# One 512-column product for the high weights of A11 and A12, with VectorE adding the two halves of the bank

## The reference, cut to what matters

```python
D_MODEL, SEQ, DEPTH = 1024, 512, 4
D_FF = int(math.ceil(8 * D_MODEL / 3 / 256) * 256)      # 2816

def _swiglu(x, w13, w2):
    h = x @ w13                       # (512, 1024) @ (1024, 5632)
    g, u = jnp.split(h, 2, axis=-1)
    return (jax.nn.silu(g) * u) @ w2

for i in range(DEPTH):
    ...
    x = _layer_norm(ALPHA * x + h, ln1_g[i], ln1_b[i])
    x = _layer_norm(ALPHA * x + _swiglu(x, ffn_w13[i], ffn_w2[i]), ln2_g[i], ln2_b[i])
```

## Time and profile before

| | |
|---|---|
| median of three runs | 2151.86 us |
| lowest and highest | 2151.69 and 2152.13 us |
| span of the profiled execution | 2150.7 us |
| PE busy | 2136.8 us, 99% |
| DVE busy | 1505.6 us, 70% |
| ACT busy | 904.9 us, 42% |
| POOL busy | 551.6 us, 26% |
| matmuls of 256 columns in the seven products (L1577 to L1579) | 3 x 2016 |
| granted TensorE clock | 0.999 of full |

### The profile page before, as it was taken

One profiled execution on the slowest core, in us unless ns is written; L12 is line 12 of the kernel. 1 busy time (PEld: TensorE's weight loads), 2 busy tenths in 40 slices (PEclk: granted clock), 3 DMA queues, 4 the chain that ended last, 5 costly groups with the idle time before them and its releaser, 6 DMA issues.

```text
span 2150.7 us, 35581 instructions
## 1 busy us (share of the span) xinstructions
PE 2136.8 (99%) x13496; PEld 1898.5 (88%) x13497; DVE 1505.6 (70%) x2118; ACT 904.9 (42%) x1594; POOL 551.6 (26%) x386
## 2 busy tenths in 40 slices
PE   9999999999999999999999999999999999999998
PEld 7777899998888988999888899988887778999987
DVE  3788688873489979888544888853538868888534
ACT  3455444442233424444323445432335554454422
POOL 0000056630030002666120166610000001666100
PEclk9999999999999999999999999999999999999999
DMA  6211323433333012343521333432232113333321
GB/s 215 69 58 51 107 81 104 113 110 116 107 99 98 1 59 79 101 116 99 177 98 50 98 99 100 117 121 96 78 117 69 49 58 100 99 99 111 126 98 59
DMA packets 256749, 204.39 MB, mean 95 GB/s; under 512 B 6256, under 2 KB 235760, under 8 KB 256608
## 3 DMA queue, kind: packets, MB, share of 16 engines
q1 hardware_dynamic: 252976, 189.42, 29.2%
q0 software_dynamic: 3632, 13.02, 1.8%
HBM read 200.32 MB, written 2.10 MB: 94 GB/s over the span
## 4 chain that ended last, share of the span: by engine, by line
PE 93%; DVE 5%; DMA 1%; issue 1%; ACT 1%; POOL 0%; DVEq 0%; POOLq 0%; SPq 0%; ACTq 0%
PE ps L1498 17%; PE ps L1500 17%; PE ps L1499 17%; PE ps L1577 11%; PE ps L1578 11%; PE ps L1579 11%; DVE hid L1263 3%; PE ps L1795 2%; PE ps L1822 2%; PE ps L1623 1%; PE ps L1807 1%; PE ps L1798 1%; PE ps L1956 0%; PE ps L2051 0%; DMA raw<-in_w 0%
## 5 line engine op out<-in xcount | busy, mean ns | idle before, releaser
L963 DVE TENSOR_TENSOR w_lo<-raw,w_hi 128x1024 fp32r<-128x1024 f32 x196 | 243.1, 1247 | 333.3 <-ACT w_hi L586 332.4
L586 ACT ACTIVATE w_hi<-raw 128x1024 fp32r<-128x1024 f32 x196 | 203.5, 1055 | 373.5 <-PE ps L1500 360.0
L1577 PE MATMUL ps<-t_hi,w_hi 128*128 128x256 f32 x1152 | 326.2, 283 | 0.2 <-DVE w_lo L1404 0.2
L1578 PE MATMUL ps<-t_lo,w_hi 128*128 128x256 f32 x1152 | 326.0, 283 | 0.0
L1579 PE MATMUL ps<-t_hi,w_lo 128*128 128x256 f32 x1152 | 326.0, 283 | 0.0
L1498 PE MATMUL ps<-w_hi,a_hi 128*128 128x512 f32 x832 | 325.9, 392 | 0.0
L1500 PE MATMUL ps<-w_hi,a_lo 128*128 128x512 f32 x832 | 323.9, 389 | 0.0
L1499 PE MATMUL ps<-w_lo,a_hi 128*128 128x512 f32 x832 | 323.8, 389 | 0.0
L653 ACT ACTIVATE w_hi<-raw 128x512 fp32r<-128x512 f32 (+1 forms) x288 | 212.5, 738 | 250.3 <-PE ps L1579 235.3
L1404 DVE TENSOR_TENSOR w_lo<-raw,w_hi 128x512 fp32r<-128x512 f32 (+1 forms) x288 | 268.1, 932 | 47.3 <-ACT w_hi L653 47.1
L1577 PE MATMUL ps<-xT_hi,w_hi 128*128 128x256 f32 x864 | 244.6, 283 | 0.0
(11 more groups left out here) (170 smaller groups left out, 4223.6 us busy)
## 6 DMA issues: line engine op xcount, KB each, us to landing
raw<-in_w SPq DMA_DIRECT2D x264, 512.0 KB, 4.1
raw<-in_wqkv SPq DMA_DIRECT2D x48, 512.0 KB, 3.8
raw<-in_pw SPq DMA_DIRECT2D x24, 512.0 KB, 4.2
raw<-in_wo SPq DMA_DIRECT2D x16, 512.0 KB, 3.2
ln_gb<-in_g POOLq DMA_DIRECT2D x8, 512.0 KB, 4.3
ln_gb<-in_b POOLq DMA_DIRECT2D x8, 512.0 KB, 5.6
x_nat<-in_x SPq DMA_DIRECT2D x4, 512.0 KB, 5.4
out<-x_nat SPq DMA_DIRECT2D x3, 512.0 KB, 2.7
```

What stands on the lines that cost most here:

```text
L586: nc.scalar.activation(weight_hi(u), raw[:, r, :], ACT.Copy).then_inc(w_hi_done, 1)
L963: nc.vector.tensor_tensor(weight_lo(u), raw[:, r, :], weight_hi(u).bitcast(f32), ALU.subtract).then_inc(w_lo_done, 1)
L1577: ms = [nc.tensor.matmul(dst, hi[:, at], x_hi, start=k == 0 and f in ("A11", "S1", "S2"), stop=False, skip_group_check=True), nc.tensor.ma ...
L1578: nc.tensor.matmul(dst, hi[:, at], x_lo, start=False, stop=False, skip_group_check=True),
```

## The change

The tiles `xT_hi` and `xT_lo` become the two halves of one tile `xT`. For A11 and A12 the two matmuls with high weights (256 columns of high tokens, 256 columns of low tokens) become one matmul of 512 columns: the product with the high tokens goes to columns 0 to 255 of bank X, that with the low tokens to columns 256 to 511. The third matmul (low weights, high tokens) still adds to columns 0 to 255. The two halves of the bank must be added afterwards: ACT copies the second half to SBUF, DVE adds the first half to it (`fold_first` for A11, `fold_head` for A12). Silu for the first 256 tokens then can't be applied by that copy, so ACT applies it later to all 512 tokens at once (`all_tokens`).

```diff
             def keep_first(p):
                 act.wait_ge(form_used, used(i, p, "A11"))
                 ...
-                nc.scalar.activation(sums_kept(i)[0][:, p % 2, :], ps[:, seven_bank(i), 0:HALF], ACT.Copy).then_inc(kept, 1)
+                nc.scalar.activation(sums_kept(i)[0][:, p % 2, :], ps[:, seven_bank(i), HALF:SEQ], ACT.Copy).then_inc(kept_half, 1)
             def first_tokens(p):
                 ...
-                nc.scalar.activation(gate[:, c % 2, 0:HALF], ps[:, seven_bank(i), 0:HALF], func).then_inc(head_done, 1)
-            def last_tokens(p):
+                nc.scalar.activation(gate[:, c % 2, 0:HALF], ps[:, seven_bank(i), HALF:SEQ], ACT.Copy).then_inc(head_half, 1)
+            def all_tokens(p):
                 c = SEVEN_FROM + p
+                act.wait_ge(head_done, SEVENS * i + p + 1)
                 act.wait_ge(c12_done, SEVENS * i + p + 1)
-                nc.scalar.activation(gate[:, c % 2, HALF:SEQ], gate[:, c % 2, HALF:SEQ], func).then_inc(gate_done, 1)
+                nc.scalar.activation(gate[:, c % 2, :], gate[:, c % 2, :], func).then_inc(gate_done, 1)
...
+            def fold_first(p):
+                dve.wait_ge(kept_half, SEVENS * i + p + 1)
+                nc.vector.tensor_tensor(firsts[:, p % 2, :], firsts[:, p % 2, :], ps[:, X, 0:HALF], ALU.add).then_inc(kept, 1)
+            def fold_head(p):
+                c = SEVEN_FROM + p
+                dve.wait_ge(head_half, SEVENS * i + p + 1)
+                nc.vector.tensor_tensor(gate[:, c % 2, 0:HALF], gate[:, c % 2, 0:HALF], ps[:, X, 0:HALF], ALU.add).then_inc(head_done, 1)
...
             form_low(0, G_S1)
+            fold_first(0)
+            fold_head(0)
             make_u2(0)
             for p in range(1, SEVENS):
                 ...
                 make_c21(p - 1)
+                fold_first(p)
                 form_low(p, G_A22)
                 make_c12(p - 1)
                 form_low(p, G_S4)
                 gating_seven(p - 1)
+                fold_head(p)
                 make_u2(p)
...
+                    if f in ("A11", "A12"):
+                        both = xT[:, :, k + (4 if f == "A12" else 0), 0:HALF]
+                        ms = [nc.tensor.matmul(ps[:, X, :].rearrange("p (h n) -> p h n", h=2), hi[:, at], both,
+                                               start=k == 0 and f == "A11", stop=False, skip_group_check=True),
+                              nc.tensor.matmul(dst, lo[:, at], both[:, 0, :], start=False, stop=k == 3, skip_group_check=True)]
```

More of the change, by code:

```diff
@@ L208, in build @@
     x_nat = sb("x_nat", [P, TB, D])
-    xT_hi = sb("xT_hi", [P, KD, SEQ], f32r)
-    xT_lo = sb("xT_lo", [P, KD, SEQ], f32r)
+    xT = sb("xT", [P, 2, KD, SEQ], f32r)
+    xT_hi, xT_lo = xT[:, 0, :, :], xT[:, 1, :, :]
     hid = sb("hid", [P, FC * SEQ])
@@ L321, in build @@
     form_lo = [sem(f"form_lo{g}") for g in range(5)]
+    kept_half, head_half = sem("kept_half"), sem("head_half")
     u2_done, u3_done, c22_done, c21_done, c12_done = (sem("u2_done"), sem("u3_done"), sem("c22_done"), sem("c21_done"),
@@ L696, in up @@
                     form_high(p, G_S4)
-                    last_tokens(p - 1)
+                    all_tokens(p - 1)
                     first_tokens(p)
@@ L703, in up @@
                 split_w(after + 1)
-                last_tokens(last)
+                all_tokens(last)
                 act.wait_ge(form_used, used(i, last, "S4"))
@@ L1575, in product @@
                     at = slice(k * P, (k + 1) * P)
+                    if f in ("A11", "A12"):
[3 more added lines that the diff above has]
+                              nc.tensor.matmul(dst, lo[:, at], both[:, 0, :], start=False, stop=k == 3, skip_group_check=True)]
+                        if k < 2 and (p, f) == (SEVENS - 1, "A11"):
+                            for m, done in zip(ms, ((w_hi_done, w_lo_done), (w_used,))[k]):
+                                m.then_inc(done, 2 * SEVENS)
+                        continue
                     x_hi, x_lo = tokens(f, k)
@@ L1579, in product @@
                           nc.tensor.matmul(dst, lo[:, at], x_hi, start=False, stop=k == 3, skip_group_check=True)]
-                    if k == 0 and (p, f) == (SEVENS - 1, "A11"):
-                        for m, done in zip(ms, (w_hi_done, w_lo_done, w_used)):
-                            m.then_inc(done, 2 * SEVENS)
                 ms[-1].then_inc(form_used, 1)
```

## The result

The changed kernel took 2172.30, 2173.32, 2174.00 and 2177.19 us, median 2173.66; the kernel before 2151.99 (median of four: the three runs of the table and one more; 2151.69 to 2154.25). The ratio is 1.0101, 95% interval 1.0087 to 1.0116: slower by 1%. The profiled execution took 2172.3 us with a span of 2170.5, against 2150.7 before, so its trace has 19.8 us to account for.

The account below looks back on a forecast made before the run. TensorE was taken to bound the kernel, 93% of the chain that ended last. 12.2 - 0.4 + 7.5 + 1.0 = +20.3 us on the profiled 2150.7 gave 2171.0, as a median of runs 2172 us; range 2161 to 2184.

Parts of the forecast that it names:

- S3 waits for u2 in the held pairs: Before S3 in 64 pairs: second fold delays u2 by 0.34 us, TensorE stands 0.30, pair 10.27 not 10.08: +12.2 us.
- The gating's end is tied to T0 by POOL: DVE's gating, held until POOL is through, ends at 7.94 us after T0, A11(p)'s first matmul; the 0.107 us gain is lost.
- Last pairs: Last pair of each layer: its gating isn't held, so it keeps the merge's gain: 4 x 0.107, -0.4 us.
- First pairs: First pair of each layer: A12(0) waits for the first fold behind the low part of S1; 1.9 us each, +7.5 us.
- Load ahead of the low part: Where a load arrives before DVE's low part, POOL goes first and DVE is held 1.2 us; +1 us allowed.
- rival B: POOL's first sum often precedes the low part of S2 and S3: 0.40 us more every second pair, 2184 us; chance 0.16.
- The merge's gain: A11 and A12: two steps of 0.120 us become one of 0.227, 0.107 a pair, 7.7 us if nothing waits.
- Rival A: Gating isn't held, the second fold is free, the 7.7 us come through: 2144 us, or 2150.5 by the skill; chance 0.06.
- Rival C: u2's reserve before S3 is larger than read, folds cost only at the layers' start: -7.3 + 7.5, 2152 us; chance 0.06.

Follow-up runs that it names:

- e2: The kernel before, products not merged, with one more addition of the folds' form directly ahead of u2 in pairs 1 to 17: 2168.10 us (1.0072).
- e3: The changed kernel with the second fold moved behind u2 in pairs 1 to 17: 2157.61 us (1.0023).
- e6: The changed kernel with POOL's first sum of a pair waiting for the low part of S2 and S3 of the pair before: 2183.46 us (1.0144).
- e7: The changed kernel with the second fold and u2 ahead of the gating in pairs 1 to 17: 2156.92 us (1.0022).
- e4: The changed kernel, each layer's first pair reordered: first fold before the low part of S1, gating behind it, second fold behind u2: 2168.43 us (1.0073).
- e1: The kernel before with only the merge into 512-column products; nothing folded, low-token part of A11 and A12 left out: 2147.54 us (0.9978).
- e5: The kernel of e1 with the 512 columns read as one piece instead of two pieces of 256: 2147.32 us (0.9976).
- e9: The changed kernel with the orders of e7 and e4, A11 and A12 issued as four wide then four narrow matmuls: 2145.35 us (0.9969).

## Why the prediction was right, and which terms were off

The forecast was 2172 us, range 2161 to 2184, and the median is 2173.7. Term by term:

- **S3 waits for u2 in the held pairs.** This was the step that carried the forecast, and it was right. Predicted: u2 at T0 + 8.20, S3 first at + 8.76 (8.83 in effect), pair 10.27. Measured: + 8.19, + 8.75, 10.253. Shown by e2 (the addition alone makes the same pair) and e3 (moving it away undoes it). Predicted +12.2 us, measured 64 x 0.173 = 11.1. The step before S3 was 0.30 and not the 0.35 that I gave as a sign, as S3 was due later by what the merge did not gain.
- **The gating's end is tied to T0 by POOL.** Shown by e6 (all is later with POOL) and e7 (0.68 us behind the sum instead of 1.79). That is why the gain of the merge was lost whole, and why its wrong size did no harm to the forecast.
- **Last pairs.** Predicted -0.4, measured 4 x (10.014 - 10.080) = -0.3.
- **First pairs.** Predicted 7.5, measured 7.05; e4 takes the wait away.
- **Load ahead of the low part.** The mechanism of rival B was there, its size between my allowance and B: 7 pairs of 10.53 to 10.57 us, some 0.29 more each (B had 0.40), and the pair after each 0.05 to 0.26 more, where B had it normal: 2.9 us in all against 1.0. DVE and POOL in one of them:

```profile
361.58 2.31 DVE L1406 TENSOR_TENSOR w_lo<-s,w_hi 128x1024 fp32r<-128x1024 f32 x1
```

```profile
361.41 1.40 POOL L524 TENSOR_TENSOR raw<-raw 128x512 f32<-128x512 f32 x1 [0.57 <-DMA raw<-in_w]
```

  The sum came 0.17 ahead, and the low part took 2.31 instead of 1.22. I had taken one row, the sum at T0 + 1.84, less 0.19. The median over the pairs did move like that, from T0 + 1.93 to + 1.71, but the sums of the kernel before spread from + 1.75 to + 3.00; 0.2 earlier, the first of them are ahead of a low part at + 1.60. And three of the seven are the second pair of a layer, where the sum starts at T0 + 1.1, right behind POOL's instruction before it: the load was there, after the wait in the first pair. That these two terms are tied I had missed. Yet in e4, without that wait, more pairs later in the layers have it. How often it happens in a given order was not settled; it hangs on when a load lands, to a tenth of a microsecond.
- **The merge's gain.** Predicted 0.107 us a pair, measured 0.067 (e1: 10.080 - 10.013), from steps of 0.234 where I took 0.227 from a stretch in which all matmuls are 512 wide. My bounds, 0.227 to 0.240, held it, but for a cause that e5 rules out, the second piece; e9 gives the order of the widths some two thirds of what was missing. The Trainium skill's figure for a matmul by itself (TensorE: Matmul & The Clock Gate, "Back-to-back issue gap"), 2.5 ns over columns / 2.4, would have given an estimated 1.4 us in e1; measured are 4.7.

That the sum came so near is in part luck. The terms give 11.1 - 0.3 + 7.05 + 2.9 us, less 0.3 for three pairs that were already longer before, 20.4 us on the span against 20.3 predicted; but the held and the first pairs were together 1.5 us under their forecast, and the loads 1.9 us over. I had also put the median of the runs 1.16 us over the traced span; it was 3.2 over it, the traced execution being the fastest of the four.

Rival A asked that the gating is not held; 57 of 72 are. Rival C asked for a reserve at S3 larger than 0.15 us; e2 rules it out. The Trainium skill's rule on the port that DVE and GpSimd share (SBUF — State Buffer, "Who interferes with whom") was borne out in all three parts. Gating and low parts, which read two SBUF operands, are held (1.79 instead of 0.68, 2.31 instead of 1.22). Folds, which read one, are not: the one at 415.07 takes its 0.42 beside POOL's first sum. And whoever comes first has the port, as the pair above shows; only where the two starts lie within 0.03 us of each other does the trace not tell who was first.

## What to carry to other kernels

Before work is moved from the engine that bounds a kernel to one that is "72% busy", look in the timeline for what it stands ahead of: here two instructions of one queue exchanged are worth 16 us, and 0.4 us of work in the right place costs nothing. Where an instruction of DVE with two SBUF operands came while GpSimd was at work, it ended 0.55 us (gating) or 1.08 us (low part of S2 and S3) after GpSimd did, nearly its own 0.68 or 1.22 us. So put what others wait for ahead of it; the instructions that took one operand from PSUM were not held. And a gain ahead of such a fixed point is no gain, until the fixed point is taken away.

## What was not expected of the hardware

With matmuls of 512 and 256 columns in turn the wide step is 0.233 to 0.241 us, one in eight 0.224, against 0.227 in a stretch of 512 columns only; it is the same whether the matmul reads one piece or two 16 KB apart (e5, e1). With four wide ones in a row it is still 0.228 to 0.236, but a pair is 0.026 us shorter (e9). The granted clock was 0.999, the 2.4 GHz level, in the changed kernel as before; from 285 to 300 us, with TensorE idle for 1.72 us in the first pair of layer 0, it was 1.00.
